# Order of the softmax pipeline, split of the gate weights and order of the attention groups in a two-block transformer kernel

## The chip, the cores and the metric

The kernel runs on one core of a Trainium2 chip, as one program for the whole computation. The metric is the device time in microseconds (us) of one execution; lower is better. Engines are called PE (TensorE), ScalarE (ACT), VectorE (DVE), GpSimd (POOL) and SP (SyncE, which here issues the weight loads).

## What is computed

Two blocks follow each other, each of two layers. The first block is an image-like transformer with a context stream: 256 latent and 256 context tokens of width 1024. Each layer normalises and modulates the tokens, projects them, runs two attentions with 8 heads each ("mla" over 96-wide heads, "na" over 64-wide heads with a bias table on the latent keys), merges both through two gates, and ends with a squared-ReLU MLP. In layer 0 the context stream attends too (here called "mlac" and "nac"). Cut to the part that the change touches:

```
s = einsum("bqhd,bkhd->bhqk", q, k) * scale ; p = softmax(s) ; y = einsum("bhqk,bkhe->bqhe", p, v)
g = sigmoid(gate_logits)                       # h @ w_in, first 2 * 1024 columns
y = g[..., :1024] * (y_mla @ w_mla_o) + g[..., 1024:] * (y_na @ w_na_o)
x = x + gate * (y @ w_out)
```

The second block (a retention, a state-space, a stick-breaking and a memory part with 4 heads each, gated and projected together) uses the same softmax routine for its memory part: 4 heads of width 128, 256 queries, 256 memory rows.

## The kernel before, in words

All arithmetic is fp32. The products with large weights are done in three passes of a reduced fp32 type: the weight chunk in the ring in SBUF is split into a high part (a copy by ScalarE, L1153 for chunks of 2048 columns, L1151 for 1024) and a low part (a subtraction by VectorE, L1588 and L1585), and PE multiplies high by high (L515), high by the low part of the activation (L516) and low by high (L517). Chunks of 2048 columns live in three ring slots and two pairs of split buffers (`w_parts`), in turn. SP refills a slot when VectorE has written the low part of the chunk in it. The first chunk of the gate phase holds gate tiles `g1` and `g2` of n=0, the second `mo` and `no` of n=0 (the two output projections) and `g1` of n=1, the third `g2`, `mo`, `no` of n=1, and so on. A tile of 8 k-steps is 24 matmuls, `mo` and `no` are 12 each.

Every engine runs its own fixed program; semaphores tie them. Nothing is scheduled: the order is the order in which the code is written.

**The attention.** A tile is one head and one half of the queries, 128 queries by 512 keys ("large", groups mla and na) or by 256 keys ("small", groups mlac, nac and the memory). Layer 0 runs the groups mla, mlac, na, nac, layer 1 mla and na, 16 tiles each, in one pipeline over turns i, with AHEAD = 3:

- PE (`softmax_attention`, L610): score of tile i (L756, L982 in the memory part), then what `between` adds, then the transpose of tile i-3 (L625), then in odd turns the value product of the head of tile i-4 (L763, L988).
- ScalarE (`softmax`, L1107): the copy of transposed tile i-4 from PSUM to `probT` (L1116), then the exponential of tile i (L1122), then what `between` adds. The copy waits for the transpose, and for the value product that used the buffer two heads ago.
- VectorE (`softmax`, L1547): bias (na only) and maximum of tile i (L1558, L1559), reciprocal and product of tile i-1 (L1563, L1565), the copy of a finished head (L1836), and what `with_tile` adds: in the na group, turns 4 to 11, the low part of the activations is moved to its place (L1842).

PSUM has 8 banks, taken in turn by `next_bank`; a bank is waited for until the event named in `until` has come.

**Behind the attention** ScalarE and VectorE split the first two gate chunks (`split_weights(("g1", l, 0))`, L1284 and L1846), then the attention output is split (L1289, L1849), and PE runs `g1`, `g2`, `mo`, `no` for n = 0 to 7. ScalarE and VectorE form the sigmoid from the gate tiles (L1304, L1545, L1130, L1132) and VectorE multiplies by `mo` and `no` (L1861). In layer 0 these tiles have 512 columns, in layer 1, where only the latent stream goes on, 256. In layer 0 VectorE also computes modulation rows there (`row_blocks`, L1634), from rows that GpSimd's queue loads once the last tile is transposed.

**The memory part of block 2** puts two gate tiles of 24 matmuls into the attention (`mem_gate`, turns 3 and 5, between score and transpose), and ScalarE and VectorE work on the split of an output weight chunk (turns 2 and 3), on the high and low parts of finished activations and on the gates' sigmoids (from turn 4) in the same turns. A gate tile's bank is free when VectorE has formed its product with the sigmoid (L2037).

## Time and profile before

| | us |
|---|---|
| time, median of 3 runs | 2126.05 (2125.37 to 2128.48) |
| profiled execution | 2126.81 |
| its span in the profile | 2125.0 |
| PE busy / VectorE busy / ScalarE busy | 2003.2 / 1351.5 / 905.0 |

The span is the time from the first to the last instruction in the trace; 1.8 us lie around it. The attention of layer 0 lies at about 264 to 404 us, that of layer 1 at 1115 to 1204, the memory attentions of block 2 at 1740 to 1761 and 2041 to 2063. Times in the rows are us from the span's start. A row of a timeline gives start, duration, engine, line, operation, output and input, the number of merged instructions, and in brackets how long the engine stood idle before it and what ended that. PEld is PE's weight load, which overlaps the matmuls (PE).

### The profile page before, as it was taken

How to read it: one execution, taken by the hardware profiler on the slowest of the kernel's cores; microseconds unless marked ns; L12 is line 12 of the kernel's file. 1: busy time of each engine (PE TensorE's matmuls, PEld its weight loads, DVE VectorE, ACT ScalarE, POOL GpSimd, SP SyncE). 2: the span in 40 equal slices, each digit the busy share in tenths (PEclk: the TensorE clock that was granted, in tenths of full speed). 3: DMA queues.
4: the chain of work that ended last, by engine and by line, in shares of the span. 5: the costliest groups of instructions: out<-in, count | busy, mean ns of one | idle time of the engine just before them, and what ended most of it. 6: DMA issues, size and time to landing. Idle time of an engine off the chain costs nothing.

```text
span 2125.0 us, 29201 instructions
## 1 busy us (share of the span) xinstructions
PE 2003.2 (94%) x11360; PEld 1630.0 (77%) x11360; DVE 1351.5 (64%) x2411; ACT 905.0 (43%) x1578; POOL 23.6 (1%) x48
## 2 busy tenths in 40 slices
PE   7999998999989999989999898999999989999987
PEld 3776354588768888878764598999999879899877
DVE  3655657576577677775446666566675665676664
ACT  3444344543342322335444564544453544443552
POOL 0000000000000000000000000000000000000000
PEclk9999999999999999999999999999999999999998
DMA  6331300144345454523121154455444324454313
GB/s 269 117 119 62 141 30 1 60 159 149 108 159 178 149 188 160 187 89 117 61 103 50 57 182 177 177 179 177 150 160 130 111 88 144 157 159 138 108 64 108
DMA packets 56327, 272.15 MB, mean 128 GB/s; under 512 B 6400, under 2 KB 7552, under 8 KB 39168
## 3 DMA queue, kind: packets, MB, share of 16 engines
q1 hardware_dynamic: 49856, 229.59, 31.5%
q0 software_dynamic: 6336, 40.70, 5.4%
q8 instruction: 92, 1.51, 0.3%
q14 instruction: 43, 0.35, 0.0%
HBM read 269.22 MB, written 1.05 MB: 127 GB/s over the span
## 4 chain that ended last, share of the span: by engine, by line
PE 71%; DVE 14%; ACT 9%; issue 6%; DMA 1%; ACTq 0%; SPq 0%; DVEq 0%
PE bank L515 15%; PE bank L517 15%; PE bank L516 15%; PE bank L763 4%; PE bank L551 4%; PE bank L756 3%; DVE small_lo L1585 2%; ACT w_parts L1153 2%; PE bank L562 2%; PE bank L1006 1%; PE bank L1008 1%; PE bank L1007 1%; PE bank L644 1%; DVE w_parts L1588 1%; DVE stat L1559 1%
## 5 line engine op out<-in xcount | busy, mean ns | idle before, releaser
L515 PE MATMUL bank<-h_hi,small_hi 128*128 128x256 f32 (+2 forms) x976 | 311.8, 320 | 11.7 <-DVE small_lo L1585 6.3
L517 PE MATMUL bank<-h_hi,small_lo 128*128 128x256 f32 (+2 forms) x976 | 301.8, 309 | 0.0
L516 PE MATMUL bank<-h_lo,small_hi 128*128 128x256 f32 (+2 forms) x976 | 301.5, 309 | 0.0
L1585 DVE TENSOR_TENSOR small_lo<-ring,small_hi 128x1024 fp32r<-128x1024 f32 (+1 forms) x180 | 214.8, 1209 | 108.1 <-ACT small_hi L1151 106.5
L1588 DVE TENSOR_TENSOR w_parts<-ring,w_parts 128x2048 fp32r<-128x2048 f32 x96 | 219.8, 2292 | 92.4 <-ACT w_parts L1153 92.3
L516 PE MATMUL bank<-h_parts,w_parts 128*128 128x512 f32 (+1 forms) x768 | 261.3, 340 | 0.0
L1153 ACT ACTIVATE w_parts<-ring 128x2048 fp32r<-128x2048 f32 x96 | 182.8, 1907 | 175.2 <-PE bank L517 175.2
L515 PE MATMUL bank<-b_parts,w_parts 128*128 128x512 f32 (+1 forms) x640 | 216.1, 338 | 1.6 <-DVE w_parts L1588 1.2
L516 PE MATMUL bank<-b_parts,w_parts 128*128 128x512 f32 (+1 forms) x640 | 215.4, 337 | 0.0
L517 PE MATMUL bank<-b_parts,w_parts 128*128 128x512 f32 (+1 forms) x640 | 215.3, 336 | 0.0
L515 PEld LDWEIGHTS bank<-h_hi,small_hi 128*128 128x128 f32 (+1 forms) x976 | 190.4, 195 | 26.5 <-issue 16.6
L516 PEld LDWEIGHTS bank<-h_lo,small_hi 128*128 128x128 f32 (+1 forms) x976 | 190.2, 195 | 11.2 <-issue 2.2
L517 PEld LDWEIGHTS bank<-h_hi,small_lo 128*128 128x128 f32 (+1 forms) x976 | 189.9, 195 | 9.2
L1151 ACT ACTIVATE small_hi<-ring 128x1024 fp32r<-128x1024 f32 (+1 forms) x180 | 182.7, 1036 | 18.3 <-DMA ring<-in_w 18.3
L515 PE MATMUL bank<-h_parts,w_parts 128*128 128x512 f32 (+1 forms) x512 | 175.2, 342 | 10.4 <-DVE h_parts L1916 7.1
L517 PE MATMUL bank<-h_parts,w_parts 128*128 128x512 f32 (+1 forms) x512 | 174.1, 340 | 0.0
L516 PEld LDWEIGHTS bank<-h_parts,w_parts 128*128 128x128 f32 x768 | 147.6, 192 | 15.7
L515 PEld LDWEIGHTS bank<-b_parts,w_parts 128*128 128x128 f32 x640 | 121.4, 190 | 15.6 <-issue 3.1
L517 PEld LDWEIGHTS bank<-b_parts,w_parts 128*128 128x128 f32 x640 | 121.4, 190 | 12.6
L516 PEld LDWEIGHTS bank<-b_parts,w_parts 128*128 128x128 f32 x640 | 121.5, 190 | 12.6
L1122 ACT ACTIVATE prob<-bank,stat 128x512 f32<-128x512 f32 (+1 forms) x112 | 66.7, 596 | 127.9 <-DVE stat L1559 127.2
L515 PEld LDWEIGHTS bank<-h_parts,w_parts 128*128 128x128 f32 x512 | 99.0, 193 | 23.2 <-issue 12.6
(253 smaller groups left out, 3886.6 us busy)
## 6 DMA issues: line engine op xcount, KB each, us to landing
ring<-in_w SPq DMA_DIRECT2D x212, 512.0 KB, 3.5
ring<-in_w SPq DMA_DIRECT2D x96, 1024.0 KB, 4.8
lowrank<-in_rows POOLq DMA_DIRECT2D x24, 1024.0 KB, 5.2
wide<-in_ada SPq DMA_DIRECT2D x8, 1024.0 KB, 12.8
prob<-in_rows POOLq DMA_DIRECT2D x16, 512.0 KB, 3.8
ring<-in_w SPq DMA_DIRECT2D x16, 288.0 KB, 2.9
lowrank<-in_bias POOLq DMA_DIRECT2D x2, 2048.0 KB, 10.1
x<-in_x SPq DMA_DIRECT2D x1, 2048.0 KB, 14.4
```

Source lines behind the costliest of these rows:

```text
L515: pe.matmul(ps, w[0][:, k, :], hi, start=k == 0, stop=False)
L516: pe.matmul(ps, w[0][:, k, :], lo, start=False, stop=False)
L517: return pe.matmul(ps, w[1][:, k, :], hi, start=False, stop=k == nk - 1)
L551: mm = pe.matmul(out, w[:, k, :], src(k), start=first and k == 0, stop=last and k == nk - 1)
L562: mm = pe.matmul(ps[:, 0:w], stationary, given("sq", (name, l, k))[:, 0:w], start=k == max(0, n - 2), stop=k == n - 1)
L756: return pe.matmul(ps[:, 0:P * nk], qs[r, a, q:q + P], ks[r, a, 0:P * nk], start=True, stop=True)
L763: mm = pe.matmul(ps[r:r + VD, 0:T], vs[:, k, VD * hd:VD * hd + VD], probT[:, hd % 2, k, :], start=k == 0, stop=k == nk - 1)
L1122: act.activation(e[:, 0:w], bank((g, "S", u))[:, 0:w], ACT.Exp, bias=stat[:, u % 4, 0:1], accum_out=stat[:, u % 4, 1:2]).then_inc(*signal( ...
L1151: act.activation(small_hi[:, pair, 0:size], small[:, slot, 0:size], ACT.Copy).then_inc(*signal("w_hi", i))
L1153: act.activation(w_parts[pair][:, 0, 0:size], ring[:, slot, 0:size], ACT.Copy).then_inc(*signal("w_hi", i))
L1585: dve.tensor_tensor(small_lo[:, slot, 0:size], small[:, slot, 0:size], small_hi[:, pair, 0:size].bitcast(F32), ALU.subtract).then_inc(*sig ...
L1588: dve.tensor_tensor(w_parts[pair][:, 1, 0:size], ring[:, slot, 0:size], w_parts[pair][:, 0, 0:size].bitcast(F32), ALU.subtract).then_inc(* ...
```

## The change

Four things change.

1. In ScalarE's `softmax` the transposed tile i-3 is copied in turn i, ahead of exponential i; before it was tile i-4. The routine is shared by the attention of block 1 and the memory attention of block 2.
2. The first two gate chunks are split in quarters of 512 columns. First chunk: ScalarE in turns 4, 6, 8, 10 of group mla, VectorE in turns 11 to 14 of it. Second chunk: ScalarE in four turns of group na (8 to 11 in layer 0, 12 to 15 in layer 1), VectorE in turns 12 to 15 of na in layer 0 and behind all tiles in layer 1. In layer 0 VectorE moves the activations' low part four turns earlier, turns 0 to 7 of na.
3. PE runs the first gate tile (`g1`, n=0) in the turn behind the last score, ahead of the last three transposes.
4. In layer 0 the groups come as mla, mlac, nac, na: the small tiles ahead of the large. GpSimd's wait for the last transpose names na accordingly.

The diff, cut where it repeats:

```
--- before.py
+++ after.py
@@ -472,9 +472,8 @@
             out = [("mla", mq, mk, mv, mla, TC, 4, 0)]
             if l == 0:
                 out.append(("mlac", mq, mk, mv, mla, 0, 2, 0))
+                out.append(("nac", nq, nk, nv, na, 0, 2, 4))
             out.append(("na", nq, nk, nv, na, TC, 4, 4))
-            if l == 0:
-                out.append(("nac", nq, nk, nv, na, 0, 2, 4))
             return out
         block = ctx.enter_context(nc.Block())
@@ -607,7 +606,7 @@
                     if a == 0:
                         half_full(mm, name, lw, i, 0)
-            def softmax_attention(tiles, until="y_copied", between=None):
+            def softmax_attention(tiles, until="y_copied", between=None, beyond=None):
                 for i in range(len(tiles) + AHEAD):
@@ -617,6 +616,8 @@
                         full(score(ps, u), g, "S", u)
                         if between:
                             between(u)
+                    if i == len(tiles) and beyond:
+                        beyond()
                     if i >= AHEAD:
                         g, u, nk, _, _ = tiles[i - AHEAD]
                         pe.wait_ge(*event("probs", g, u))
@@ -766,19 +767,23 @@
                     return [((gname, l), u, nk, score, value) for u in range(2 * NH)]
-                softmax_attention([t for g in groups(l) for t in head_tiles(*g[0:7])])
-
-
                 h_hi, h_lo = (h_parts[:, a, :, t0:TT] for a in range(2))
                 gate_hi = h_hi1[:, :, t0:TT]
                 b_hi, b_lo = (b_parts[:, a, :, t0:TT] for a in range(2))
+                def turn_tile(name, n, hi, lo, by, ready=None):
+                    ps = next_bank(name, l, n, until=(by, name, l, n))
+                    full(split_linear(ps[:, 0:cw], (name, l, n), hi, lo, ready if n == 0 else None), name, l, n)
+                softmax_attention([t for g in groups(l) for t in head_tiles(*g[0:7])],
+                                  beyond=lambda: turn_tile("g1", 0, gate_hi, h_lo, "gate_exp", ("h_lo", "h", l)))
                 for n in range(KT):
-                    for name, hi, lo, by, ready in (
-                            ("g1", gate_hi, h_lo, "gate_exp", ("h_lo", "h", l)), ("g2", gate_hi, h_lo, "gate_exp", None),
-                            ("mo", b_hi, b_lo, "merged", ("b_lo", "y", l)),
-                            ("no", b_hi[:, 4:8, :], b_lo[:, 4:8, :], "merged", ("b_lo", "y4", l))):
-                        ps = next_bank(name, l, n, until=(by, name, l, n))
-                        full(split_linear(ps[:, 0:cw], (name, l, n), hi, lo, ready if n == 0 else None), name, l, n)
+                    if n:
+                        turn_tile("g1", n, gate_hi, h_lo, "gate_exp")
+                    turn_tile("g2", n, gate_hi, h_lo, "gate_exp")
+                    turn_tile("mo", n, b_hi, b_lo, "merged", ("b_lo", "y", l))
+                    turn_tile("no", n, b_hi[:, 4:8, :], b_lo[:, 4:8, :], "merged", ("b_lo", "y4", l))
                 for n in range(KT):
                     ps = next_bank("out", l, n, until=("x_attn", l, n))
                     full(split_linear(ps[:, 0:cw], ("out", l, n), yg_hi[:, :, t0:TT], yg_lo[:, :, t0:TT],
@@ -1055,7 +1060,7 @@
                 for b in range(ROWS, 48 if l == 0 else 0):
                     if b < ROWS + 2:
-                        pool.wait_ge(*event("psum_full", ("nac", l), "T", 2 * NH - 1))
+                        pool.wait_ge(*event("psum_full", ("na", l), "T", 2 * NH - 1))
                     else:
                         pool.wait_ge(*event("row_used", 0, b - 2))
                     pool.dma_start(prob_all[:, 2 * (b % 2):2 * (b % 2) + 2, :].rearrange("p a t -> p (a t)"),
@@ -1106,12 +1111,12 @@
             def softmax(tiles, between=None):
-                for i in range(len(tiles) + AHEAD + 1):
-                    if i > AHEAD:
-                        g, v, w = tiles[i - AHEAD - 1]
+                for i in range(len(tiles) + AHEAD):
+                    if i >= AHEAD:
+                        g, v, w = tiles[i - AHEAD]
                         act.wait_ge(*event("psum_full", g, "T", v))
-                        if i - AHEAD - 1 >= 4:
-                            last, u, _ = tiles[i - AHEAD - 5]
+                        if i - AHEAD >= 4:
+                            last, u, _ = tiles[i - AHEAD - 4]
                             act.wait_ge(*event("psum_full", last, "Y", u // 2))
                         act.activation(probT[:, (v // 2) % 2, 0:w // P, P * (v % 2):P * (v % 2) + P],
                                            bank((g, "T", v))[:, 0:w].rearrange("p (k q) -> p k q", q=P), ACT.Copy).then_inc(*signal("probT", g, v))
@@ -1152,6 +1157,21 @@
                         continue
                     act.activation(w_parts[pair][:, 0, 0:size], ring[:, slot, 0:size], ACT.Copy).then_inc(*signal("w_hi", i))
+            def split_quarter(i, q):
+                _, slot, _, pair, before = slots[i]
+                cols = slice(SLOT // 4 * q, SLOT // 4 * q + SLOT // 4)
+                if q == 0:
+                    split_next["at"] = i + 1
+                    act.wait_ge(*event(loaded(i), i))
+                    for j in before or []:
+                        act.wait_ge(*event(*chunk_used(j)))
+                    if before is None:
+                        act.wait_ge(*event("h_lo", "h", l_now[0], KT - 1))
+                ins = act.activation(w_parts[pair][:, 0, cols], ring[:, slot, cols], ACT.Copy)
+                if q == 3:
+                    ins.then_inc(*signal("w_hi", i))
             act.preload_act_table_set("natural_log_exp_and_others")
             act.wait_ge(*event("par_in"))
@@ -1280,12 +1300,17 @@
                     if i:
                         rms(("mq", i - 1), l, QK, QK, cw, ("normed", ("mq", i - 1), l, 0))
-                softmax([((g[0], l), u, P * g[6]) for g in groups(l) for u in range(2 * NH)])
-                split_weights(("g1", l, 0))
-                last = ("na" if l else "nac", l)
+                def split_gate(g, u):
+                    if g[0] == "mla" and u in (4, 6, 8, 10):
+                        split_quarter(place["g1", l, 0][0], u // 2 - 2)
+                    if g[0] == "na" and 0 <= u - 8 - 4 * l < 4:
+                        split_quarter(place["mo", l, 0][0], u - 8 - 4 * l)
+                softmax([((g[0], l), u, P * g[6]) for g in groups(l) for u in range(2 * NH)], split_gate)
                 for k in range(KT):
-                    act.wait_ge(*event("y_copied", last, NH - 1))
+                    act.wait_ge(*event("y_copied", ("na", l), NH - 1))
                     act.activation(b_parts[:, 0, k, t0:TT], y_heads(k)[:, t0:TT], ACT.Copy).then_inc(*signal("b_hi", "y", l, k))
                 def split_yg(n):
@@ -1587,6 +1612,18 @@
                         continue
                     dve.tensor_tensor(w_parts[pair][:, 1, 0:size], ring[:, slot, 0:size],
                                       w_parts[pair][:, 0, 0:size].bitcast(F32), ALU.subtract).then_inc(*signal("w_lo", i))
+            def split_quarter(i, q):
+                _, slot, _, pair, _ = slots[i]
+                cols = slice(SLOT // 4 * q, SLOT // 4 * q + SLOT // 4)
+                if q == 0:
+                    split_next["at"] = i + 1
+                    dve.wait_ge(*event("w_hi", i))
+                ins = dve.tensor_tensor(w_parts[pair][:, 1, cols], ring[:, slot, cols],
+                                        w_parts[pair][:, 0, cols].bitcast(F32), ALU.subtract)
+                if q == 3:
+                    ins.then_inc(*signal("w_lo", i))
             def low_part(parts, k, src, cols, name, *key):
@@ -1836,14 +1873,21 @@
                     dve.tensor_copy(y_heads(y0 + hd // 2)[r, qcol:qcol + T], bank((g, "Y", hd))[r, 0:T]).then_inc(*signal("y_copied", g, hd))
                 def with_tile(g, u):
-                    if g[0] == "na" and u == 4:
+                    if g[0] == "na" and u == 4 * l:
                         dve.wait_ge(*event("psum_full", ("mla" if l else "mlac", l), "Y", NH - 1))
-                    if g[0] == "na" and 4 <= u < 4 + KT:
-                        dve.tensor_copy(h_parts[:, 1, u - 4, t0:TT], h_lo1[:, u - 4, t0:TT]).then_inc(*signal("h_lo", "h", l, u - 4))
+                    k = u - 4 * l
+                    if g[0] == "na" and 0 <= k < KT:
+                        dve.tensor_copy(h_parts[:, 1, k, t0:TT], h_lo1[:, k, t0:TT]).then_inc(*signal("h_lo", "h", l, k))
+                    if g[0] == "mla" and u in (11, 12, 13, 14):
+                        split_quarter(place["g1", l, 0][0], u - 11)
+                    if g[0] == "na" and l == 0 and u >= 12:
+                        split_quarter(place["mo", l, 0][0], u - 12)
                 softmax([((g[0], l), u, P * g[6]) for g in groups(l) for u in range(2 * NH)], y_out, with_tile)
-
-                split_weights(("g1", l, 0))
+                if l:
+                    for q in range(4):
+                        split_quarter(place["mo", l, 0][0], q)
                 for k in range(KT):
                     dve.wait_ge(*event("b_hi", "y", l, k))
                     ins = dve.tensor_tensor(b_parts[:, 1, k, t0:TT], y_heads(k)[:, t0:TT],
```

Where it puts the instructions. ScalarE's program at the start of the memory attention of block 2, layer 0; `prob,stat<-bank,stat` is an exponential, `probT<-bank` the copy of a transposed tile, `small_hi<-ring` the high part of an output weight chunk, `tmp<-bank` the exponential of gate tile 14. Before:

```order
L1122 ACTIVATE prob,stat<-bank,stat 128x256 x4
L1151 ACTIVATE small_hi<-ring 128x1024
L1116 ACTIVATE probT<-bank 128x2x128
L1122 ACTIVATE prob,stat<-bank,stat 128x256
L1405 ACTIVATE y_hi<-wide 128x256
L1411 ACTIVATE tmp<-bank 128x256
L1116 ACTIVATE probT<-bank 128x2x128
L1122 ACTIVATE prob,stat<-bank,stat 128x256
```

and changed:

```order
L1127 ACTIVATE prob,stat<-bank,stat 128x256 x3
L1121 ACTIVATE probT<-bank 128x2x128
L1127 ACTIVATE prob,stat<-bank,stat 128x256
L1156 ACTIVATE small_hi<-ring 128x1024
L1121 ACTIVATE probT<-bank 128x2x128
L1127 ACTIVATE prob,stat<-bank,stat 128x256
L1430 ACTIVATE y_hi<-wide 128x256
L1436 ACTIVATE tmp<-bank 128x256
L1121 ACTIVATE probT<-bank 128x2x128
```

The first copy moved ahead of the fourth exponential and of the chunk's high part. The same shift, with the quarters (`w_parts_49<-ring 128x512`), stands at the start of the attention of block 1, ScalarE again. Before:

```order
L1122 ACTIVATE prob,stat<-bank,stat 128x512 x4
L1116 ACTIVATE probT<-bank 128x4x128
L1122 ACTIVATE prob,stat<-bank,stat 128x512
L1116 ACTIVATE probT<-bank 128x4x128
L1122 ACTIVATE prob,stat<-bank,stat 128x512
```

and changed:

```order
L1127 ACTIVATE prob,stat<-bank,stat 128x512 x3
L1121 ACTIVATE probT<-bank 128x4x128
L1127 ACTIVATE prob,stat<-bank,stat 128x512
L1121 ACTIVATE probT<-bank 128x4x128
L1127 ACTIVATE prob,stat<-bank,stat 128x512
L1172 ACTIVATE w_parts_49<-ring 128x512
L1121 ACTIVATE probT<-bank 128x4x128
```

VectorE's program at the end of the attention of layer 1; `sq<-bank` is the copy of a head, `w_parts` a chunk's low part, `b_parts` the low part of the attention output, the `tmp` rows belong to the gates. Before:

```order
L1836 COPY sq<-bank 64x256 x3
L1588 TENSOR_TENSOR w_parts_49<-ring,w_parts_49 128x2048
L1588 TENSOR_TENSOR w_parts_50<-ring,w_parts_50 128x2048
L1849 TENSOR_TENSOR b_parts<-tmp,b_parts 128x256 x4
L1849 TENSOR_TENSOR b_parts<-sq,b_parts 128x256 x4
L1545 TENSOR_SCALAR tmp<-tmp 128x256 x2
L1861 TENSOR_TENSOR tmp<-tmp,bank 128x256
L1588 TENSOR_TENSOR w_parts_49<-ring,w_parts_49 128x2048
```

and changed:

```order
L1873 COPY sq<-bank 64x256 x3
L1623 TENSOR_TENSOR w_parts_50<-ring,w_parts_50 128x512 x4
L1893 TENSOR_TENSOR b_parts<-tmp,b_parts 128x256 x4
L1893 TENSOR_TENSOR b_parts<-sq,b_parts 128x256 x4
L1570 TENSOR_SCALAR tmp<-tmp 128x256 x2
L1905 TENSOR_TENSOR tmp<-tmp,bank 128x256
L1613 TENSOR_TENSOR w_parts_49<-ring,w_parts_49 128x2048
```

The first chunk's low part is gone from here, the second's is still here in quarters, and the third chunk's stands behind the same rows as before. On PE at the same place, the last transposes (`con,prob`) and value products (`probT,wide`), before:

```order
L763 MATMUL bank<-probT,wide 64x256 x4
L625 MATMUL bank<-con,prob 128x128 x8
L763 MATMUL bank<-probT,wide 64x256 x4
L625 MATMUL bank<-con,prob 128x128 x4
L763 MATMUL bank<-probT,wide 64x256 x4
L515 MATMUL bank<-h_hi_52,w_parts_49 128x256
```

and changed, where the 24 matmuls of `g1` (two are shown) start behind the value product that goes ahead of the last transposes:

```order
L626 MATMUL bank<-con,prob 128x128 x4
L764 MATMUL bank<-probT,wide 64x256 x4
L514 MATMUL bank<-h_hi_52,w_parts_49 128x256
L515 MATMUL bank<-h_parts,w_parts_49 128x256
```

The gate tile moved from behind the last value product to ahead of the last three transposes.

## Rows read from the trace of the kernel before

**Rows 1.** Page's busy line; na group, layer 0: length, PE, PEld, DVE, ACT, POOL, clock, DMA.

```profile
PE 2003.2 (94%) x11360; PEld 1630.0 (77%) x11360; DVE 1351.5 (64%) x2411; ACT 905.0 (43%) x1578; POOL 23.6 (1%) x48
...
328.00:372.00 44.00, 40.15 (x151) 18.24 (x150) 33.45 (x85) 20.66 (x54) 0.00 (x0) 1.00 0.00 1
```

**Rows 2.** Who waited for line L1116, whole span: us in total, times.

```profile
  PEld bank L763: 29.9, 48
  PE bank L763: 18.0, 40
```

**Rows 3.** Timeline of one pair of tiles in group mla, layer 0, PE and ScalarE.

```profile
284.70 1.94 PE L763 MATMUL bank<-probT,wide 128*64 128x256 f32 x8 [0.40 <-ACT probT L1116]
...
289.20 0.59 ACT L1116 ACTIVATE probT<-bank 128x512 f32<-128x512 f32 x1
...
289.84 1.94 PE L763 MATMUL bank<-probT,wide 128*64 128x256 f32 x8 [0.40 <-ACT probT L1116]
```

**Rows 4.** Timeline, value products on PE in groups mlac, na and nac of layer 0.

```profile
312.87 1.08 PE L763 MATMUL bank<-probT,wide 128*64 128x256 f32 x4 [0.57 <-ACT probT L1116]
...
316.02 1.08 PE L763 MATMUL bank<-probT,wide 128*64 128x256 f32 x4 [0.57 <-ACT probT L1116]
...
353.63 1.94 PE L763 MATMUL bank<-probT,wide 128*64 128x256 f32 x8 [0.38 <-ACT probT L1116]
...
386.12 1.08 PE L763 MATMUL bank<-probT,wide 128*64 128x256 f32 x4
```

**Rows 5.** Timeline of PE at the end of the attention of layer 0.

```profile
402.57 1.08 PE L763 MATMUL bank<-probT,wide 128*64 128x256 f32 x4 [0.47 <-ACT probT L1116]
...
406.74 0.76 PE L515 MATMUL bank<-h_hi,w_parts 128*128 128x512 f32 x1 [3.09 <-issue]
```

**Rows 6.** Stretches of the gate phases: window, length, PE busy, granted clock, DMA.

```profile
406.70:410.20 3.50, 3.46 (x9) 0.52 0.72 250
410.20:425.00 14.80, 14.80 (x66) 1.00 0.21 88
1215.00:1230.00 15.00, 15.00 (x129) 1.00 0.45 146
```

**Rows 7.** Timeline behind the attention of layer 1, all engines.

```profile
1202.14 1.94 PE L763 MATMUL bank<-probT,wide 128*64 128x256 f32 x8 [0.69 <-ACT probT L1116]
...
1204.58 4.49 DVE L1588 TENSOR_TENSOR w_parts<-ring,w_parts 128x2048 fp32r<-128x2048 f32 x2
...
1206.97 0.36 PE L515 MATMUL bank<-h_hi,w_parts 128*128 128x256 f32 x1 [2.89 <-issue]
...
1208.99 1.43 DVE L1849 TENSOR_TENSOR b_parts<-tmp,b_parts 128x256 fp32r<-128x256 f32 x4
...
1214.01 1.90 ACT L1153 ACTIVATE w_parts<-ring 128x2048 fp32r<-128x2048 f32 x1
...
1215.93 2.29 DVE L1588 TENSOR_TENSOR w_parts<-ring,w_parts 128x2048 fp32r<-128x2048 f32 x1 [1.18 <-ACT w_parts L1153]
...
1218.41 0.32 PE L515 MATMUL bank<-h_hi,w_parts 128*128 128x256 f32 x1
```

**Rows 8.** Timeline of the memory attention of block 2, layer 0, all engines.

```profile
1743.86 0.48 ACT L1122 ACTIVATE prob<-bank,stat 128x256 f32<-128x256 f32 x1 [0.23 <-DVE stat L1559]
...
1744.32 1.05 ACT L1151 ACTIVATE small_hi<-ring 128x1024 fp32r<-128x1024 f32 x1
...
1744.93 0.38 PE L625 MATMUL bank<-con,prob 128*128 128x128 f32 x2
...
1745.35 0.39 ACT L1116 ACTIVATE probT<-bank 128x256 f32<-128x256 f32 x1
...
1745.40 1.23 DVE L1585 TENSOR_TENSOR small_lo<-ring,small_hi 128x1024 fp32r<-128x1024 f32 x1 [1.18 <-ACT small_hi L1151]
...
1746.54 0.42 DVE L1559 TENSOR_REDUCE stat<-bank 128x1 f32<-128x256 f32 x1
...
1751.14 0.70 PE L982 MATMUL bank<-wide 128*128 128x256 f32 x2 [0.79 <-DVE yT L2037]
```

## Prediction

> **What bounds the kernel now.** Read first the busy line: TensorE (PE) works in 94% of the span, so a change pays where PE stands idle or at the low clock, and nowhere else [rows 1]. Then ask who PE waited for: the value product (L763) waited 18.0 us in 40 places for ScalarE's copy of the transposed tile (L1116) [rows 2]. The timeline shows why. In turn i PE does score i, transpose i-3 and, in odd turns, the value product of tile i-4. ScalarE copies transpose i-4 in its own turn i, thus only behind its exponential of tile i-1, which itself had to wait for a score and a maximum. In the first group a pair of tiles takes 5.14 us, and 0.40 of it is PE waiting for that copy [rows 3]. In the small context tiles the wait is 0.57, in the neighbourhood tiles 0.38, and in the small neighbourhood tiles PE shows none [rows 4].
>
> The other holes are at the end of each layer's attention. The split of the gate weights (ScalarE high part, VectorE low part) comes only behind the last tile: PE starts the first gate tile after 3.09 us of idle in layer 0 [rows 5] and after 2.89 in layer 1 [rows 7]. In layer 0 it also starts at the low one of the two clock levels: granted 0.52 in the stretch behind the hole, 1.00 from 410.2 [rows 6]. In layer 1 the clock stayed high: the 96 matmuls from 1206.97 to 1218.41 take 0.119 us each [rows 7], as in a stretch at 1.00 (129 in 15.0) [rows 6].
>
> **Part 1, copy in its own turn.** ScalarE copies transpose i-3 ahead of exponential i, a whole turn before the value product asks for it. Is there room? ScalarE is busy 20.7 of 44.0 us in the neighbourhood group of layer 0, VectorE 33.5, PE 40.2 [rows 1]. In a large pair: score, transpose ends 1.6 to 1.7 us in, copy 0.59, exponential 0.69; the copy ends a good half microsecond before the value product, whose turn comes about 2.9 to 3.4 us in. The exponential starts later by at most a few tenths, and is wanted by PE only three turns later. So PE's wait goes away: 18.0 us. What stays is the end of each layer, where no exponential separates the two anyway: the last value product still waits 0.69 in layer 1 [rows 7] and 0.47 in layer 0 [rows 5], and by the same latency I leave 0.25 for the one before, together 1.7. Because the large tiles now come last in layer 0 too, its last wait becomes 0.69 (0.2 more). Gain 18.0 - 1.7 - 0.2 = **16.1**. Low bound: half of it, 8, if VectorE, which carries the most in the neighbourhood tiles, falls behind. High bound: the weight loads of L763 waited 29.9 us in 48 places [rows 2], 11.9 more than the products; if loads may now run beneath the transposes, 11.9 more. I take the low of the two figures since the score behind a value product, which waits for nobody, does not start earlier either.
>
> The Trainium skill bears on this: TensorE: Matmul & The Clock Gate, Part 2, "Step-by-step", states that the queue pulls a weight load ahead of running matmuls when row groups don't conflict or it goes to the background buffer. By that rule the gain would be 28.0; by the rows of the products it is 16.1. No row here shows a value product without its wait, so this stands as a rival below.
>
> **Part 2, weights in quarters.** The first chunk (gate tiles 0) is split by ScalarE in turns 4, 6, 8, 10 and by VectorE in turns 11 to 14 of the first group; the second (output projections 0 and gate tile 1) in the last group, VectorE's share of it in layer 1 only behind the last head. Two whole chunks take VectorE 4.49 us, so four quarters take at least 2.25; by the 256-column subtracts (four in 1.43) a 512-column quarter could take up to 0.72, 2.9 for four [rows 7]. I take 0.60, 2.4 for four. On ScalarE a whole is 1.90 [rows 7], a quarter about 0.5 to 0.6. Two turns of a large pair have 5.14 us minus the 0.40, ScalarE needs 2 x (0.59 + 0.69) and one quarter: 3.2. VectorE in the neighbourhood group has 44.0 - 33.5 = 10.5 free, minus 3.3 for PE's shorter turns, and takes 2.4 more in layer 0. Hidden, cost 0; if that cover is gone, 4 chunks at 2.4 to 2.9 are the price. SP's queue is moved too: it waits for the low part before it refills the slot, so the fourth chunk is asked for inside the attention, where DMA moves nothing [rows 1]. Cost 0.
>
> **Part 3, layer 0 behind the attention.** The split no longer stands before the gate tile: 3.09 us of idle go. The nine matmuls in 3.50 us at 0.52 would take 9 x 14.8/66 = 2.0 at full clock [rows 6]: 1.5 more. Gate tile 0 (24 matmuls) moves ahead of the last transposes; as PE work it is neither more nor less. Behind the last value product there is now the second gate tile, 24 x 14.8/66 = 5.4 us, and under it fit the head's copy, the first high part and the first low part (about 2 us). Gain **4.6**, bounds 3.1 and 4.6.
>
> **Part 4, layer 1 behind the attention.** Tiles are half as wide: 24 matmuls take 24 x 15.0/129 = 2.8 us [rows 6]. From the last value product's end, t = 0 (1204.1): VectorE copies the head until 0.5, splits the second chunk until 2.9, then subtracts eight low parts, 8 x 0.34 = 2.7, until 5.6. PE runs gate tile g2 until 2.8, waits 0.5 for the first low part, then mo and no (1.4 each) and g1 of n=1, until 9.0. The next tile needs the third chunk. Its chain is: low parts 5.6, adding one 0.3 (as a 256-column subtract), logarithm and exponential 0.8 (one exponential of that width is 0.48 [rows 8], and the second starts a little before the first is out), ScalarE's split 1.9, VectorE's split 2.3, and 0.1 to 0.2 on semaphores, less where they overlap: 10.9 us. So PE waits 1.9. Before, the same tile began at 1218.4 [rows 7], that is 14.3 after; now 10.9, plus the 2.8 of g1 that went ahead: 13.7. Gain **0.6** instead of 2.9: gate tile 0 used to cover this chain, and it has been taken away from here. In layer 0 the same chain has tiles of 5.4 us over it and just fits, as before. Bounds 0 and 2.9.
>
> **Part 5, the memory attention.** The same ScalarE routine serves it, twice, and there the new order adds a wait. In turns 3 and 5 PE puts a gate tile of some 2.9 us between score and transpose. Before, ScalarE's turn 3 was: exponential 3 at 1743.86, split of an output weight chunk at 1744.32; the copy followed at 1745.35, when transpose 0 (1744.93) was done [rows 8]. Now copy 0 comes first: it ends at 1745.7 and exponential 3 at 1746.2, and the split starts then, 1.9 later than before. Queued behind it are VectorE's low part (1745.40 to 1746.6) and behind that its maximum 4 (1746.54), which exponential 4, the gate's logistic and product 14 follow; PE already waits for that product, 0.79 at 1751.14 [rows 8]. Nothing on this path has slack, so the wait grows by 1.9, and 0.1 comes at the next gate: 2.0 in each layer, **-3.9**. Bounds: 0 if slack hides there, -5.8 if the other gate tile adds half as much again.
>
> **Sum.** 16.1 + 4.6 + 0.6 - 3.9 = 17.4. The profiled execution took 2126.81 (span 2125.0 and 1.8 around it), 0.76 above the median 2126.05. From the median: **2108.6 us**.
>
> **The rivals.** (A) Weight loads run ahead beneath the transposes: 11.9 more, 2096.7. For: the loads' idle time is longer than the products'. Against: the loads of the score wait too, with "issue" only. (B) The memory attention loses nothing: 2104.7. Against: its path is a chain without gaps. (C) VectorE becomes the bound in the neighbourhood tiles, with adding of the bias, casts and quarters: half of part 1 goes, 8 less: 2116.7. (D) Slower: exponential i now waits for transpose i-3, which PE runs only behind score i. If the three turns of distance are used up, each small turn becomes serial: score 0.7, transpose 0.4, copy 0.4, exponential with its sum 0.6 [rows 8], 2.1 us against half a pair of 3.15 now [rows 4], 0.5 more over 32 + 16 small tiles, 24 us; the large ones then gain nothing. With +5.2 from parts 3 and 4 and -3.9, the time is 2126.05 + 24 - 1.3 = 2148.8. It decides only if VectorE's product with the reciprocal comes three turns late; it now comes one turn behind the exponential. (E) The copies change nothing, since PE's own switch between tile shapes fills the gap: parts 3 to 5 leave 1.3: 2124.8.
>
> **Chances.** Forecast 0.62 (own range 2105 to 2112), A 0.10, B 0.09, C 0.11, D 0.04, E 0.04. The range leaves out D, E and A: 2101 to 2118. About 0.2% (4.3 us) is what a measurement of this kernel can tell from no change. Faster by more: forecast, A, B, C: 0.92. Within: E, 0.04. Slower: D, 0.04.
>
> **What the changed profile would show.** Waits of L763 for the copy down from 18.0 to 2 or 3 us; a pair of the first group at 4.7 instead of 5.14, if 4.5 then A is right. No hole and clock 1.00 at the first gate tile of layer 0. In layer 1 a wait of about 2 us at the second tile g2 for the low part of the third chunk. In the memory attention the wait for the gate product grows from 0.8 to 2.7. If pairs keep 5.1 us, part 1 is wrong, and the name of the releaser says whether C, D or E.

## The result and the profile after

| | before | after |
|---|---|---|
| median, us | 2125.89 (4 runs, 2125.37 to 2128.48) | 2104.78 (4 runs, 2097.07 to 2109.97) |
| profiled execution, us | 2126.81 | 2109.97 |
| its span and mean granted clock | 2125.0, 0.980 | 2107.8, 0.978 |
| ratio of the means | | 0.9895, 95% interval 0.9864 to 0.9927 |

The kernel became 21.1 us faster; 17.4 were forecast, and 2104.78 stands inside the range. Its times spread over 13 us, those of before over 3, and they go with the clock: the four runs of 2109.97, 2105.34, 2104.23 and 2097.07 us had 0.978, 0.981, 0.982 and 0.984 as mean granted clock. A second set of runs, on another chip, gave 2105.56 against 2125.75 (0.9908, 0.9894 to 0.9921), so 20.2 us. Below, a landmark is one and the same instruction looked up in two profiles. In the changed kernel ScalarE's copy stands on L1121, its exponential on L1127, the quarters on L1172 (ScalarE) and L1623 (VectorE), the whole splits on L1158 and L1613, scores, transposes and value products on L757, L626 and L764, the memory attention's scores and products on L987 and L993, and the gate product on L2081.

The busy line of the page answers to the first of [rows 1]: less idle PE, the same work.

```profile
PE 2004.4 (95%) x11360; PEld 1630.3 (77%) x11360; DVE 1352.0 (64%) x2423; ACT 909.2 (43%) x1590; POOL 23.6 (1%) x48
```

Who waited for the copy (L1121), over the whole span; us, times. It answers to [rows 2], where PE's value product waited 18.0 in 40 places:

```profile
  PEld bank L764: 4.3, 12
...
  PE bank L764: 1.9, 4
```

What is left are four waits, two at the end of each layer's attention. A pair of the first group, PE and then ScalarE, in the place of [rows 3] (start, length, engine, line):

```profile
282.59 1.94 PE L764 MATMUL bank<-probT,wide 128*64 128x256 f32 x8
...
286.72 0.60 PE L626 MATMUL bank<-con,prob 128*128 128x128 f32 x4
287.25 1.94 PE L764 MATMUL bank<-probT,wide 128*64 128x256 f32 x8
```

```profile
286.06 0.60 ACT L1121 ACTIVATE probT<-bank 128x512 f32<-128x512 f32 x1 [1.73 <-PE bank L626]
286.55 0.68 ACT L1127 ACTIVATE prob<-bank,stat 128x512 f32<-128x512 f32 x1
...
287.21 0.63 ACT L1172 ACTIVATE w_parts<-ring 128x512 fp32r<-128x512 f32 x1
```

The pair takes 4.66 us instead of 5.14, the product has no wait, and the copy is over at 286.66, 0.59 ahead of it. A quarter of the weights (0.63) stands behind the exponential and delays nobody. The other groups: mlac 3.15 to 2.51, nac 3.15 to 3.00, na 5.60 to 5.15 (start of one value product to the start of the next).

The end of the attention of layer 0, PE, and the stretch behind it (window, length, PE busy, granted clock, DMA), in the place of [rows 5] and of the first of [rows 6]:

```profile
390.77 1.94 PE L764 MATMUL bank<-probT,wide 128*64 128x256 f32 x8 [0.25 <-ACT probT L1121]
392.64 0.66 PE L626 MATMUL bank<-con,prob 128*128 128x128 f32 x4
393.98 1.94 PE L764 MATMUL bank<-probT,wide 128*64 128x256 f32 x8 [0.69 <-ACT probT L1121]
```

```profile
396.00:406.00 10.00, 10.00 (x44) 1.00 0.22 88
```

The hole of 3.09 and the low clock behind it are gone. Behind the attention of layer 1 ([rows 7]) PE's waits, 1155 to 1204 us, are the one for the third chunk (L1613), forecast as 1.9, and the one for the first low part (L1893), forecast as 0.5; the wait in the middle is that of the last two value products:

```profile
PE bank L514 <- DVE w_parts L1613: 1.6, 1, 1.6
PE bank L764 <- ACT probT L1121: 0.9, 2, 0.7
PE bank L514 <- DVE b_parts L1893: 0.5, 1, 0.5
```

And in the memory attention of layer 0 of block 2 (1725 to 1745 us), where [rows 8] had 0.79 for the first of them and 2.7 was forecast:

```profile
PE bank L987 <- DVE yT L2081: 2.6, 1, 2.6
PE bank L626 <- DVE yT L2081: 1.9, 1, 1.9
PE bank L993 <- ACT probT L1121: 0.7, 2, 0.5
```

### The profile page after: what moved, and what is told of

Its sections match the earlier page's. It is cut to its first block, busy times and chain, and to the rows that moved or that the text cites. A ratio compares the mean times of both kernels' runs of the same rounds, so it can differ in the third digit from the quotient of the medians.

```text
span 2107.8 us, 29225 instructions
## 1 busy us (share of the span) xinstructions
PE 2004.4 (95%) x11360; PEld 1630.3 (77%) x11360; DVE 1352.0 (64%) x2423; ACT 909.2 (43%) x1590; POOL 23.6 (1%) x48
## 4 chain that ended last, share of the span: by engine, by line
PE 75%; DVE 12%; ACT 7%; issue 5%; DMA 1%; ACTq 0%; SPq 0%; DVEq 0%
PE bank L514 15%; PE bank L516 15%; PE bank L515 15%; PE bank L757 4%; PE bank L550 4%; PE bank L764 4%; ACT w_parts L1158 2%; DVE small_lo L1610 2%; PE bank L626 2%; PE bank L561 2%; PE bank L1011 1%; PE bank L1013 1%; PE bank L645 1%; PE bank L1012 1%; DVE w_parts L1613 1%
## 5 line engine op out<-in xcount | busy, mean ns | idle before, releaser
L1613 DVE TENSOR_TENSOR w_parts<-ring,w_parts 128x2048 fp32r<-128x2048 f32 x92 | 210.8, 2291 | 92.9 <-ACT w_parts L1158 92.9
L1158 ACT ACTIVATE w_parts<-ring 128x2048 fp32r<-128x2048 f32 x92 | 175.4, 1907 | 175.5 <-PE bank L516 175.5
L1671 DVE SCALAR_TENSOR_TENSOR prob<-lowrank,c_rows 128x1024 f32<-128x1024 f32 x96 | 113.4, 1219 | 0.0
## 6 DMA issues: line engine op xcount, KB each, us to landing
wide<-in_ada SPq DMA_DIRECT2D x8, 1024.0 KB, 12.9
```

The costliest lines, as they stand in the source:

```text
L1158: act.activation(w_parts[pair][:, 0, 0:size], ring[:, slot, 0:size], ACT.Copy).then_inc(*signal("w_hi", i))
L1613: dve.tensor_tensor(w_parts[pair][:, 1, 0:size], ring[:, slot, 0:size], w_parts[pair][:, 0, 0:size].bitcast(F32), ALU.subtract).then_inc(* ...
L1671: ins = dve.scalar_tensor_tensor((product1 if l else product)[:, s, :], w, 1.0, c_rows[:, s, :], ALU.mult, ALU.mult, accum_out=mod_sum[:, ...
```

## The experiments

Theory: the parts add up as forecast, with 16.1 for the copies revised to 20 after a look at the pairs. Rivals: the order of the groups and the early splits do the work; the memory attention loses nothing; the tile that was moved hides something. No run changes the order of the groups by itself. Each run has its own runs of the kernel before beside it, on the same chip; runs of one chip stand together.

### The copies alone

Two kernels, both the kernel before with the new order of copies. The edit of ScalarE's routine, where `late=1` is the old order:

```diff
-            def softmax(tiles, between=None):
+            def softmax(tiles, between=None, late=0):
-                for i in range(len(tiles) + AHEAD + 1):
-                    if i > AHEAD:
-                        g, v, w = tiles[i - AHEAD - 1]
+                for i in range(len(tiles) + AHEAD + late):
+                    if i >= AHEAD + late:
+                        g, v, w = tiles[i - AHEAD - late]
...
-                        if i - AHEAD - 1 >= 4:
-                            last, u, _ = tiles[i - AHEAD - 5]
+                        if i - AHEAD - late >= 4:
+                            last, u, _ = tiles[i - AHEAD - late - 4]
```

The one keeps the old order in the memory attention:

```diff
-                softmax([(("memory", l), u, T) for u in range(8)], with_memory)
+                softmax([(("memory", l), u, T) for u in range(8)], with_memory, late=1)
```

> The kernel before, with one edit: in the attention of both layers of block 1 ScalarE copies transpose i-3 ahead of exponential i. The memory attention keeps the old order, and no weight split and no gate tile is moved. Theory as recorded (part 1 alone): 16.1 us, from 2125.9 to 2109.8. Revised theory, from the pairs of the changed kernel (mla 5.14 to 4.67, mlac 3.15 to 2.51, nac 3.15 to 3.00, na 5.60 to 5.15; 16, 8, 8 and 16 pairs): 7.5 + 5.1 + 1.2 + 7.2 = 21.0, less 1 at the ends: 20.0, that is 2105.9. Rival (the gain of the changed kernel comes from the order of the groups and the weights split early, and the copies only take PE's waits off the record): under 8 us, 2118 or more.

Measured: 2106.59 (2104.20 to 2108.20) against 2125.75, ratio 0.9911 (0.9898 to 0.9925): **19.2 us** by the copies of block 1 alone, near the revised figure and more than the 16.1 on record. The rival of under 8 falls. From the first score to the last value product layer 0 took 138.16 us before and 125.26 here (12.9 less); in layer 1, counted from the score at 1121.59 (here 1110.43) to the last value product at 1202.14 (here 1184.08), it was 80.55 and is 73.65 (6.9 less): 19.8. Something of it is given back behind the attention of layer 0. The hole is still there, and more of the work behind it runs at the low clock. PE, window, length, busy (matmuls), granted clock, DMA; this kernel and then the one before:

```profile
392.00:398.00 6.00, 4.07 (x10) 0.59 0.84 318
398.00:402.00 4.00, 4.00 (x15) 0.76 0.63 262
```

```profile
406.00:410.00 4.00, 3.26 (x8) 0.58 0.74 262
410.00:412.00 2.00, 2.00 (x10) 0.99 1.03 426
```

The low level is half of the full clock, so twice what is missing to 1.00, times the length, is the time spent at it: (0.41 x 6 + 0.24 x 4) x 2 = 6.8 us here and (0.42 x 4 + 0.01 x 2) x 2 = 3.4 before. That takes back up to 1.7 us of the gain, behind a hole of the same 3.09 us.

The other has the new order in the memory attention as well.

> The kernel before, with the copy in its own turn wherever that routine is used, the memory attention too; nothing else moved. Against the run with block 1 alone: the theory that the memory attention loses (the wait for the gate product grows by 1.8 in each layer) makes it slower by 3.9 as recorded, by 3.7 from the landmarks of the changed kernel (2.6 and 1.1): 2109.6. Rival (the memory attention loses nothing, and what is seen there in the changed kernel is the low clock): the same as block 1 alone within 1 us, and the waits of PE for the gate product stay at 0.8.

Measured: 2113.11 (2110.76 to 2116.18), ratio 0.9943 (0.9929 to 0.9957): **6.5 us slower** than block 1 alone. The rival falls, and the term of 3.9 was too small. PE's waits of the memory attention of layer 0 (1715 to 1765 us), the kernel with block 1 alone and then this one:

```profile
PE bank L988 <- ACT probT L1116: 1.9, 3, 1.2
PE bank L625 <- DVE yT L2037: 1.6, 1, 1.6
...
PE bank L982 <- DVE yT L2037: 0.8, 1, 0.8
```

```profile
PE bank L625 <- DVE yT L2037: 2.9, 1, 2.9
PE bank L982 <- DVE yT L2037: 2.6, 1, 2.6
...
PE bank L988 <- ACT probT L1116: 0.5, 1, 0.5
```

Waits for the gate product rise from 2.4 to 5.5, waits for the copy fall from 1.9 to 0.5: 1.7 net, near the 2.0 on record. Still PE needs 3.0 us more from its last matmuls ahead of this attention to those behind it (16.3 and 19.3 us between the same two), because the longer stall is followed by more time at the low clock (PE, again block 1 alone and then this one):

```profile
1740.00:1748.00 8.00, 7.27 (x40) 0.79 0.01 2
```

```profile
1740.00:1748.00 8.00, 5.62 (x15) 0.59 0.01 2
```

In layer 1 the two profiles part by another 2.9, but that the order of copies costs this there is not shown: the waits grow by 0.5 net (4.1 and 0.7 against 2.4 and 1.9), and between the same two matmuls the kernel before, with the old order, takes 42.1 us, this one 42.0 and block 1 alone 39.2. A further 3.2 of this one profile come at 1902, at a place that neither kernel changed (last section).

### The changed kernel, with the old order in the memory attention

The same two edits, made to the changed kernel.

> The changed kernel, with the old order of copies in the memory attention only. If the new order costs there: faster than the changed kernel by 3.7 to 3.9 us (about 2101), PE's two waits for the gate product 0.8 instead of 2.6, clock 1.00 behind the first of them. Rival (it costs nothing): within 1 us of the changed kernel, 2104.8.

> The changed kernel as it is, so that the others stand beside it on one chip. Median expected near 2104.8, runs between 2097 and 2110: if the spread comes from where the low clock falls, the fast runs have a mean granted clock of 0.984 and the slow ones of 0.978; the spread of the kernel before stays at 3 us.

Measured: the changed kernel 2105.56 (2105.09 to 2106.47), with the old memory order 2097.96 (2095.27 to 2099.97), ratio to before 0.9871 (0.9857 to 0.9884). So one edit in the memory attention gives **7.6 us** between the medians, about twice what was forecast, and this version beats both kernels. Its runs and those of the changed kernel on that chip don't overlap. The runs of the changed kernel had a clock of 0.979 to 0.981, those of this version 0.983 to 0.985. Of what was expected of the changed kernel's spread nothing came: its four runs lay within 1.4 us.

But not all of the 7.6 can be a loss in the memory attention. PE runs the same 11360 matmuls in every kernel, so a stretch can be named by their numbers. Its length in us (numbers; time in the changed kernel's second profile):

| matmuls | what | old memory order | changed, 2nd | changed, 1st | block 1 alone | all copies |
|---|---|---|---|---|---|---|
| 3701 to 4501, 912 to 1076 | ahead of the attention of layer 1 | 161.7 | 163.4 | 163.4 | 163.4 | 163.1 |
| 4501 to 5001, 1076 to 1195 | with that attention | 117.9 | 119.6 | 119.5 | 119.6 | 121.1 |
| 8867 to 8931, 1722 to 1741 | memory attention, layer 0 | 16.3 | 18.6 | 20.3 | 16.3 | 19.3 |
| 10061 to 10151, 1890 to 1904 | products of 8 columns (last section) | 13.7 | 13.6 | 15.3 | 12.1 | 15.3 |
| 10791 to 10986, 2002 to 2045 | memory attention, layer 1 | 42.8 | 43.2 | 43.2 | 39.2 | 42.0 |

Of the 6.5 us between the profile of this version and the second of the changed kernel, 3.4 arise in the first two stretches, ahead of any memory attention and where both kernels have the same program: the low clock lasts 3.4 us at 939 and 3.4 at 1099 in this version, 10.2 and 6.8 at the same two places in both profiles of the changed kernel. Why it does is not known. The memory attention of layer 0 costs 2.3 of the 6.5 (4.0 in the first profile, 3.0 in the pair before), that of layer 1 0.4.

ScalarE and VectorE show the mechanism as it was forecast. First the old order (this version), then the new (the changed kernel, in its profile of the second set); exponential 3 is the last L1127 ahead of the split:

```profile
1714.58 0.48 ACT L1127 ACTIVATE prob<-bank,stat 128x256 f32<-128x256 f32 x1 [0.23 <-DVE stat L1584]
...
1715.04 1.05 ACT L1156 ACTIVATE small_hi<-ring 128x1024 fp32r<-128x1024 f32 x1
...
1716.07 0.38 ACT L1121 ACTIVATE probT<-bank 128x256 f32<-128x256 f32 x1
1716.12 1.23 DVE L1610 TENSOR_TENSOR small_lo<-ring,small_hi 128x1024 fp32r<-128x1024 f32 x1 [1.18 <-ACT small_hi L1156]
```

```profile
1718.40 0.38 ACT L1121 ACTIVATE probT<-bank 128x256 f32<-128x256 f32 x1 [1.72 <-PE bank L626]
...
1718.68 0.47 ACT L1127 ACTIVATE prob<-bank,stat 128x256 f32<-128x256 f32 x1
...
1719.13 1.06 ACT L1156 ACTIVATE small_hi<-ring 128x1024 fp32r<-128x1024 f32 x1
...
1720.22 1.23 DVE L1610 TENSOR_TENSOR small_lo<-ring,small_hi 128x1024 fp32r<-128x1024 f32 x1 [2.95 <-ACT small_hi L1156]
```

In the new order ScalarE stands 1.72 before the copy, for transposes that PE runs behind a gate tile, and everything queued behind it is late: VectorE waits 2.95 for the high part instead of 1.18.

### Everything but the copies

The changed kernel, with `late=1` in both calls of ScalarE's routine:

```diff
-                softmax([((g[0], l), u, P * g[6]) for g in groups(l) for u in range(2 * NH)], split_gate)
+                softmax([((g[0], l), u, P * g[6]) for g in groups(l) for u in range(2 * NH)], split_gate, late=1)
```

> The changed kernel with the old order of copies in every attention: what is left is the order of the groups, the splits in quarters and the gate tile ahead (parts 2 to 4). As recorded these give 4.6 + 0.6 = 5.2, from 2125.75 to 2120.6. The runs before this say more: the changed kernel stands 7.5 us below the kernel before with own-turn copies everywhere, and the version with the old memory order 8.6 below block 1 alone, of which some 2.4 are the low clock behind the holes, which was shorter in the kernel before; so 5 to 6 is expected, and no low clock in the stretch behind the attention of layer 0. Rival (the parts help each other): under 3 us. PE's waits for the copy come back: 18 us or a little less.

Measured: 2123.29 (11 runs, 2120.28 to 2126.86) against 2125.21 (15 runs), ratio 0.9990 (0.9981 to 0.9999): 1.9 us, not 5 to 6. **The parts do help each other**, which was the rival. PE now waits 23.8 us in 40 places for the copy, more than the 18.0 of before:

```profile
  PE bank L764: 23.8, 40
```

and the timeline shows where. ScalarE, and a value product of a pair that has a quarter in it and one that has none:

```profile
278.17 0.69 ACT L1127 ACTIVATE prob<-bank,stat 128x512 f32<-128x512 f32 x1 [2.72 <-DVE stat L1584]
...
278.85 0.62 ACT L1172 ACTIVATE w_parts<-ring 128x512 fp32r<-128x512 f32 x1
279.37 0.58 ACT L1121 ACTIVATE probT<-bank 128x512 f32<-128x512 f32 x1
```

```profile
291.31 1.94 PE L764 MATMUL bank<-probT,wide 128*64 128x256 f32 x8 [0.92 <-ACT probT L1121]
296.45 0.86 PE L764 MATMUL bank<-probT,wide 128*64 128x256 f32 x3 [0.40 <-ACT probT L1121]
```

In the old order a quarter stands between the exponential and the copy that PE waits for, and costs its pair 0.52 us. That holds for 4 pairs of the first group and 2 of the last in each layer: 12 x 0.52 = 6.2, and by the sum of the waits 23.8 - 18.0 = 5.8. In the new order it costs nothing. With the old memory order throughout, the four corners are 2125.5 (before), 2106.6 (copies), 2123.3 (the rest) and 2098.0 (both): 18.9, 2.2 and 27.5, so 6.4 come only with the two together. The 5.8 to 6.2 of the quarters account for nearly all of it. In the profiles the stretches with the two attentions of block 1 (matmuls 961 to 1981 and 4501 to 5001) give 4.3 and 2.9 by the same sum, the whole spans only 3.6: the low clock falls differently elsewhere.

### The tail of layer 1

Three kernels start from the version with the old memory order (2097.96). The first moves VectorE's quarters:

```diff
                 def y_out(g, hd):
...
+                    if l == 1 and (g[0], hd) == ("na", 6):
+                        for q in range(4):
+                            split_quarter(place["mo", l, 0][0], q)
                     dve.wait_ge(*event("psum_full", g, "Y", hd))
...
-                if l:
-                    for q in range(4):
-                        split_quarter(place["mo", l, 0][0], q)
```

> The changed kernel with the old memory order, and VectorE's four quarters of the second chunk of layer 1 placed ahead of its copy of head 6, where it stood idle for 5.0 us, instead of behind head 7. Theory of part 4 (the chain from the last head to the third chunk sets PE's waits of 0.5 and 1.6): the chain begins 2.5 earlier, both waits go, 2.0 us faster than the old memory order alone (2098.0): 2096.0. Rival (ScalarE's high parts or the gates' own chain take over): the wait for the third chunk stays over 1 us and the gain is under 1.

Measured: 2095.81 (2095.04 to 2098.68), ratio 0.9862 (0.9849 to 0.9876), and in a later set, on another chip, 2098.29 (2095.38 to 2104.94), 0.9873 (0.9854 to 0.9893). The intervals don't tell it from its base; the profile does. VectorE at the end of layer 1:

```profile
1172.71 2.50 DVE L1623 TENSOR_TENSOR w_parts<-ring,w_parts 128x512 fp32r<-128x512 f32 x4
...
1180.88 0.43 DVE L1876 COPY sq<-bank 64x256 f32<-64x256 f32 x1 [2.80 <-PE bank L764]
1181.79 1.43 DVE L1892 TENSOR_TENSOR b_parts<-tmp,b_parts 128x256 fp32r<-128x256 f32 x4 [0.48 <-ACT b_parts L1314]
```

The low parts start 0.9 behind the last head's copy, not 2.9, and of PE's 1.6 and 0.5 only 0.4 is left:

```profile
PE bank L514 <- DVE w_parts L1613: 0.4, 1, 0.4
```

The landmarks of the two profiles part by 1.9 us there, for 2.0 expected. The second puts the gate tile back:

```diff
                 softmax_attention([t for g in groups(l) for t in head_tiles(*g[0:7])],
-                                  beyond=lambda: turn_tile("g1", 0, gate_hi, h_lo, "gate_exp", ("h_lo", "h", l)))
+                                  )
                 for n in range(KT):
-                    if n:
-                        turn_tile("g1", n, gate_hi, h_lo, "gate_exp")
+                    turn_tile("g1", n, gate_hi, h_lo, "gate_exp", ("h_lo", "h", l))
```

> The changed kernel with the old memory order, and gate tile g1 of n = 0 behind the attention again in both layers; the early splits stay. Theory of part 4 (the tile was cover for the chain to the third chunk, and is missing there): PE's waits of 0.5 and 1.6 in layer 1 go, layer 0 is unchanged (its tiles of 5.4 us cover the chain either way, and the last two value products still wait 0.25 and 0.69): 2.1 us faster than the old memory order alone: 2095.9. Rival (the tile among the last turns hides something there): slower by 1 to 3 us, with longer waits of the last transposes or value products.

Measured: 2096.38 (2095.33 to 2097.10), ratio 0.9861 (0.9846 to 0.9876); 1.6 below its base. Both waits behind layer 1 are gone, the tail's 0.25 and 0.69 stay, and the landmarks part by 1.4 in layer 1 and by 0.5 the other way in layer 0. So it is the early split that fills the hole of 3.09, not the tile among the last turns; that tile gained at most 0.5 in layer 0 and uncovered a chain in layer 1. The rival falls.

The third does all four quarters of a split in one turn: ScalarE in turn 8 of mla and 10 or 14 of na, VectorE in turn 12 and 13, as in

```diff
-                    if g[0] == "mla" and u in (4, 6, 8, 10):
-                        split_quarter(place["g1", l, 0][0], u // 2 - 2)
+                    if g[0] == "mla" and u == 8:
+                        for q in range(4):
+                            split_quarter(place["g1", l, 0][0], q)
```

> The changed kernel with the old memory order, and the four quarters of each split in one turn instead of one per turn (ScalarE turn 8 of mla and turn 10 or 14 of na, VectorE turn 12 of mla and 13 of na in layer 0). If quarters matter: an exponential or a product with the reciprocal is then 2.4 us late, more than its pair has free, and PE waits for it up to 1.5 us at each of the seven places: 3 to 8 us slower than 2098.0. If three turns of distance swallow it (rival): within 1 us of it, and part 2 could have been left as whole splits.

Measured: 2099.27 (2098.41 to 2100.70), ratio 0.9877 (0.9863 to 0.9890); 1.3 above its base, with intervals that overlap. Its profile has no wait more than its base, and one pair of 4.77 instead of 4.67. ScalarE carries 2.18 us at once and catches up within three turns:

```profile
282.03 2.18 ACT L1172 ACTIVATE w_parts<-ring 128x512 fp32r<-128x512 f32 x4
284.10 0.59 ACT L1121 ACTIVATE probT<-bank 128x512 f32<-128x512 f32 x1
```

3 to 8 us are excluded; whether 1 us is lost is not settled. With the copies in their own turn the quarters hardly matter.

### The tile ahead of the last product, and the splits ahead of the memory attention's copies

Both start from the version with the quarters in the tail, which ran beside them once more.

```diff
-                    if i == len(tiles) and beyond:
-                        beyond()
...
+                if beyond:
+                    beyond()
                 one_value(tiles[-1], until)
```

> The version with the old memory order and the quarters in the tail (2095.8), and the gate tile ahead of the very last value product, behind the last transposes, instead of ahead of transpose 13. It then covers ScalarE's last copy: the last value product of both layers no longer waits 0.69. The tile's place in the chain to the third chunk is the same (it was ahead of the last value product before). Expected 1.4 faster: 2094.4; the wait of 0.25 for the value product before it stays. Rival (something else takes the place: the last transposes wait for the product with the reciprocal, since the tile no longer stands ahead of them): no gain, or slower by up to 1.

> The version with the old memory order and the quarters in the tail once more, so that the two others stand beside it on one chip. Expected 2095.8 within 1.5; where its profile differs from its own first one, the difference is the place of the stretches at the low clock alone, which bounds what a comparison of two profiles can say.

Measured: 2097.78 (2097.51 to 2099.11), ratio 0.9868 (0.9853 to 0.9883), beside 2098.29 for its base. The wait of 0.69 is gone in both layers and nothing took its place: from the last value product of a full pair to the end of the last one there pass 13.21 us in layer 0 (383.62 to 396.83) against 13.96, and 0.8 less in layer 1. But a gain of 1.5 is below what these medians tell apart. The base itself spread over 9.6 us here, with its slowest run at a clock of 0.977 and its fastest at 0.983, and of its two profiles, of one and the same program, the second is 3.6 us behind the first at 1684 us and 2.2 ahead of it at the end. That is the bound on such comparisons.

The other has the tile late too, goes back to the copies in their own turn in the memory attention and moves both splits, on ScalarE and on VectorE:

```diff
-                    if u in (2, 3):
-                        split_weights(("out2", lw, 0, u % 2), 1)
+                    if u in (1, 2):
+                        split_weights(("out2", lw, 0, u - 1), 1)
```

> As tile_late, but with own-turn copies in the memory attention, and ScalarE's and VectorE's splits of the output weights moved from turns 2 and 3 to turns 1 and 2. Tests the mechanism of part 5. If the first wait for the gate product (2.6 against 0.8) is long because the split is queued behind copy and exponential of turn 3, it falls to 1.3 or less (what is left: exponential 3 behind the copy, 0.5), and half the loss of 7 us comes back: 2094.4 plus 0 to 3. Rival (the exponential behind the copy that waits for the transposes behind PE's gate tile is the whole cause): the wait stays above 2.2 and the time at 2094.4 plus 6 to 7.

Measured: 2105.61 (2099.21 to 2106.44), ratio 0.9893 (0.9876 to 0.9910): 7.8 above tile_late, near the rival's 6 to 7. The time can't decide, though: of the 8.9 us between the two profiles 3.2 come from matmul 3701 to 4501 (166.2 us against 163.1) and 3.2 from 10061 to 10151 (15.3 against 12.1), where the programs are the same, and 2.4 from the memory attention of layer 0 (18.6 against 16.3). The waits say half and half (1712 to 1736 us):

```profile
PE bank L624 <- DVE yT L2080: 2.9, 1, 2.9
PE bank L987 <- DVE yT L2080: 1.6, 1, 1.6
PE bank L993 <- ACT probT L1121: 0.7, 2, 0.5
```

The first wait fell from 2.6 to 1.6: 1.0 of it was the split in the queue. The second, 1.6 in the old order and 1.9 in the changed kernel, is 2.9, and the two together are 4.5 as in the changed kernel: moving the split moved the wait. The timeline has a reason: ScalarE's turn 5 stands before a copy in the same way and the gate's logistic is queued behind it. So the split in the queue lengthened the first wait, and the copy that waits for transposes behind a gate tile (idle 0.77 and 1.33 us in turns 3 and 5) keeps the sum; with such a tile between score and transpose the old order did better in every pair of kernels.

## Why the prediction was right, and where not

- **What bounds the kernel.** Right. PE's waits for the copy went from 18.0 to 1.9, the kernel gained, and a pair went to 4.66 (4.7 was named).
- **Part 1, 16.1, measured 19.8 in the two attentions.** The mechanism held, and the term was mis-sized. The step that failed was to take the idle time written beside the value product [rows 2 to 4] for the whole of what the copy cost. Take starts instead. In the last group of layer 0 of before the last transposes of a pair start at 385.60 and the product at 386.12 [rows 4], 0.52 later and with no wait shown; in the changed kernel it is 334.65 and 335.01, 0.36. The transposes are written down as 0.44 long but hold PE for 0.36 only, so idle time counted from their modelled end is too short by 0.07 in a pair, and a rest of 0.08 bears no mark. 36 pairs that lose their wait x 0.07 and 7 pairs without a mark x 0.15 are 3.6: with the 16.1, and the 0.2 that was taken off for a new order of the groups, which the kernel with the copies alone doesn't have, 19.9. The Trainium skill (TensorE: Matmul & The Clock Gate, Part 2, "Step-by-step") says that after the last column of a matmul the wavefront still has some 128 cycles to drain; at 2.4 GHz that is an estimate of 0.05 us, near the 0.07. No run here shows that the two are the same thing.
- **The row that had the answer.** The weight loads (PEld) of the value product are marked as waiting in all 48 pairs, also where the product bears no mark, and the prediction had their 29.9 us at hand [rows 2]. With the copies alone 4.1 are left behind the copy, in 12 places, and the other 36 loads stand idle 0.17 each with nothing to wait for (who waited for L1116, and what ended the idle time ahead of L763):

```profile
  PEld bank L763: 4.1, 12
...
  issue: 6.1, 36
```

So 29.9 - 4.1 - 6.1 = 19.7, and 19.8 was measured. The sentence of the prediction that no row shows a value product without its wait misread the same pairs: the last of [rows 4] bears none, and its load stood idle 0.32 us.
- **Rival A**, weight loads ahead, asked for pairs of 4.5. They take 4.66, the loads of L764 have 4.3 us of waits left, and the copies gave 19.8 and not 28.0. The trace doesn't bear out at this place the rule of the Trainium skill (TensorE: Matmul & The Clock Gate, Part 2, "Step-by-step") that loads are pulled ahead: the first load of a value product starts with the product, also where its copy was long done.
- **Part 2, 0.** Right, and for a reason that the text did not see: only the new order makes it so. In the old order the same quarters cost 5.8 to 6.2 (see the corners). The forecast put them at nothing for the room on the engines in a pair; room is not enough when the quarter stands ahead of what PE waits for.
- **Part 3, 4.6.** From PE's first score to its matmul at 930.4 us of before, the changed kernel gained 17.7: 12.9 for the copies, so 4.8. Seen from the copies alone, which gained 11.8 by the same count, it is 5.8, since there the low clock behind the hole lasted longer.
- **Part 4, 0.6.** Waits of 1.9 and 0.5 forecast, 1.6 and 0.5 measured. By the landmarks layer 1 gained 6.7 in the changed kernel, 0.2 less than the 6.9 of the copies, and 1.6 more with the old memory order than with the copies alone; the low clock falls differently in each (6.8 us of it at 1098 in the changed kernel, 3.4 with the old memory order), and 0.6 lies between the two. The chain to the third chunk is as described: 2.0 of slack given to it took the waits away.
- **Part 5, -3.9; -6.5 and -7.6 between the medians.** The mechanism held, and the sizes did not. The first wait was right (2.7 forecast, 2.6). Over gate product and copy together the waits of a layer grew by 1.7 and 0.5 with the copies alone, and by 1.1 and 0.9 in the changed kernel (4.4 and 0.7 against 2.4 and 1.6; 4.4 and 0.5 against 2.4 and 1.6), where 2.0 each was taken: the wait for the copy itself shrinks, which the forecast left out. The step that failed was to price a stall as idle time alone: a stall grown from 0.8 to 2.6 also brought low clock, 1.2 us more in layer 0. What the profiles show in the two memory attentions is 5.9, 4.3 and 2.7 in three pairs of profiles. What is more than that between the medians came at places with the same program and its cause is open. The upper bound, 5.8, was not wide enough for the medians.
- **The sum.** 19.2 (copies) + 8.6 (the rest on top of them) - 7.6 (memory) = 20.2, what the second set of the changed kernel shows; 16.1 + 5.2 - 3.9 was forecast. Errors of 3.1 and 3.4 one way and 3.7 the other left 2.8: that the total was nearer than its terms is luck. So is the place of 2104.78: it is the price of rival B (2104.7), which is false, and the 2105 to 2112 given as the forecast's own range just misses it.
- **Rivals B, C, D, E.** B falls by two pairs of kernels, by the waits more than by the times. C and D fall by the pairs of nac and na, which became shorter by 0.15 and 0.45; E by the 19.2.

## What to carry to other kernels

Put the instruction for which the bounding engine waits first in its turn, ahead of work that is wanted later: it saved 19 us here, and it also decides what filler costs (a quarter of 0.6 us was free behind it and cost its pair 0.52 ahead of it). Look at every user of a shared routine: where the turn's first instruction waits for something that stands behind a long tile on the other engine, the same order is a loss; here two calls of eleven turns took back 6.5 of 19.2 us by the medians, and 2.3 to 4.0 in layer 0's call by the timeline. And to see what an instruction costs the engine that waits for it, compare start to start with a place where it does not wait, since idle time behind pipelined matmuls is under-stated; or take the idle time of its weight load, less what that load shows where nothing holds it. Before a difference of medians is called the price of an edit, see in the profiles whether it arises behind the edit.
